# Stage steps ahead of conversions, root-mean-square by token, one output conversion a slot, and attention one slot sooner, in a four-layer kernel on one core

## The reference

```
layer 0 (AB):  y = rms_norm(x) @ w_in; split into a gated linear attention (GLA, 4 heads, dk 128, dv 256)
               and a forgetting attention (8 heads of 128)
    o = gla_chunked(q, k, v, log_a)
    o = o * rsqrt(mean(o*o over dv) + 1e-6) * head_g        # per token and head
    o_gla = o * silu(gate)
    x = x + concat(o_gla, o_fox) @ w_out
layer 1 (C):   u, gate = rms_norm(x) @ w_in; z = gelu(s5_ssm(u)); z *= sigmoid(z @ glu_w + b)
               x = x + (z * silu(gate)) @ w_out
layers 2, 3:   proj = rms_norm(x) @ w_in (6160 columns), split into
    ssd branch (16 heads of 64, chunks of 128), rmsnorm over 1024, weight ssd_norm_w
    conformer:  u = a*sigmoid(g); 31-tap causal conv; silu(layernorm(u over 512)) * silu(z)
    attention:  4 heads, difference of two softmaxes, o = rmsnorm(o over 128, subln) * (1 - lambda_init) * silu(z)
    x = x + concat(y_ssd, y_cfm, y_att) @ w_out
```

## Time and profile before

| | us |
|---|---|
| median of 3 runs | 3405.67 |
| the profiled execution | 3409.92 |
| its span | 3408.1 |
| PE busy (matmul) | 3331.7 (98%) |
| DVE busy | 2139.3 (63%) |
| ACT busy | 1245.7 (37%) |
| DMA share of 16 engines, hardware queue | 50.4% |

### The profile page before, as it was taken

How to read it: one execution, slowest core, us unless ns; L and a number is a source line. 1 busy time by engine, 2 the same in 40 slices (tenths; PEclk the granted TensorE clock), 3 DMA queues, 4 the chain that set the end, 5 groups by cost and what they waited for, 6 DMA issues and landing times.

```text
span 3408.1 us, 43449 instructions
## 1 busy us (share of the span) xinstructions
PE 3331.7 (98%) x16066; PEld 2685.1 (79%) x16066; DVE 2139.3 (63%) x3149; ACT 1245.7 (37%) x1933; POOL 121.6 (4%) x84
## 2 busy tenths in 40 slices
PE   8999999999999999899999999998999999999899
PEld 7887887878888888788888887786778888777677
DVE  5665667686765655434273776666756477666774
ACT  4333324454342233323142226324434223532542
POOL 3000000000020000000020000000002000000000
PEclk9999999999999999999999999998999999999999
DMA  5433345576766666555453444444447354444445
GB/s 173 131 116 121 119 133 184 190 252 233 250 245 199 191 196 194 188 173 206 146 185 119 150 138 155 140 158 148 148 152 250 107 176 143 134 145 155 151 155 207
DMA packets 293233, 575.66 MB, mean 169 GB/s; under 512 B 63392, under 2 KB 107168, under 8 KB 293024
## 3 DMA queue, kind: packets, MB, share of 16 engines
q1 hardware_dynamic: 293024, 572.90, 50.4%
HBM read 440.66 MB, written 132.12 MB: 168 GB/s over the span
## 4 chain that ended last, share of the span: by engine, by line
PE 86%; DVE 7%; ACT 2%; DVEq 2%; DMA 2%; issue 1%; SPq 0%; ACTq 0%
PE bank L557 64%; PE bank L556 12%; DMA convert_in<-mix 1%; DVE weights_low L472 1%; PE bank L1990 1%; PE bank L1572 1%; PE bank L1098 1%; ACT weights_high L403 1%; PE bank L736 1%; DVEq L2592 1%; PE bank L1391 1%; PE bank L1595 1%; PE bank L2296 1%; PE bank L1428 1%; DVE act_low L543 0%
## 5 line engine op out<-in xcount | busy, mean ns | idle before, releaser
L557 PE MATMUL bank<-act_high,weights_high 128*128 128x512 f32 x3584 | 1432.4, 400 | 25.1 <-DVE act_low L540 11.1
L557 PE MATMUL bank<-act_low,weights_high 128*128 128x512 f32 x3584 | 1405.4, 392 | 0.0
L472 DVE TENSOR_TENSOR weights_low<-weights_raw,weights_high 128x1024 fp32r<-128x1024 f32 x528 | 655.9, 1243 | 807.0 <-ACT weights_high L403 796.9
L403 ACT ACTIVATE weights_high<-weights_raw 128x1024 fp32r<-128x1024 f32 x528 | 558.4, 1058 | 1468.5 <-PE bank L557 1220.4
L557 PE MATMUL bank<-act_high,weights_low 128*128 128x512 f32 x3584 | 963.1, 389 | 0.0
L557 PEld LDWEIGHTS bank<-act_high,weights_high 128*128 128x128 f32 x3584 | 678.7, 189 | 184.1 <-issue 24.1
L557 PEld LDWEIGHTS bank<-act_low,weights_high 128*128 128x128 f32 x3584 | 678.9, 189 | 138.4 <-issue 2.9
L557 PEld LDWEIGHTS bank<-act_high,weights_low 128*128 128x128 f32 x3584 | 672.7, 188 | 140.1
L556 PE MATMUL bank<-weights_high,act_high 128*128 128x512 f32 x640 | 253.9, 397 | 3.9 <-DVE stream_out L501 3.1
L556 PE MATMUL bank<-weights_high,act_low 128*128 128x512 f32 x640 | 249.3, 390 | 0.0
L2088 DVE SCALAR_TENSOR_TENSOR residual_in<-residual_in,arena 128x512 f32<-128x512 f32 x240 | 182.1, 759 | 20.2 <-issue 1.5
(11 more groups left out here) (325 smaller groups left out, 2644.4 us busy)
## 6 DMA issues: line engine op xcount, KB each, us to landing
weights_raw<-in_w_all SPq DMA_DIRECT2D x528, 512.0 KB, 3.4
convert_in<-mix SPq DMA_DIRECT2D x80, 256.0 KB, 4.0
fm_b<-stream_out SPq DMA_DIRECT2D x72, 256.0 KB, 3.0
mix<-arena SPq DMA_DIRECT2D x64, 256.0 KB, 3.3
x_part<-stream_out SPq DMA_DIRECT2D x48, 256.0 KB, 4.1
residual_in<-x_part SPq DMA_DIRECT2D x48, 256.0 KB, 5.6
x<-stream_out SPq DMA_DIRECT2D x48, 256.0 KB, 5.4
convert_in<-x SPq DMA_DIRECT2D x48, 256.0 KB, 4.0
```

The costliest lines, as they stand in the source:

```text
L403: e.activation(WH[:, t % 3, :], RAW[:, t % 3, :], ACT.Copy).then_inc(wh_ready, 1)
L472: e.tensor_tensor(WL[:, t % 3, :], RAW[:, t % 3, :], WH[:, t % 3, :].bitcast(F32), ALU.subtract).then_inc(wl_ready, 1)
L557: return e.matmul(bank[s][:, :], a[:, s * P:(s + 1) * P], h, start=start, stop=stop)
```

## The change

- ACT runs `take(t)` before the conversions of the slot, and in slots after a gated pass it converts the weights t+2 first and applies silu or sigmoid after (`late`).
- DVE runs `take(t)` before the conversions in the slots outside `STAGE_FIRST` (in those the stages were first already). The scaling by the ssd norm leaves `convert_dve` and is done one slot before its conversion, ahead of `take` (`scale_dve`); SP loads those blocks two slots ahead.
- The three norms work by token on 4 values a partition, like `stat_*`: one-column sums, root and reciprocal of 128x4, a broadcast copy (`spread`), a product with the identity (`cast`). The multiplications are put in another order.
- `ATT_START` becomes 88 + 6h, `att_pre` moves from slot 84 to 83, and with `ATT_START` the conversions of k = 12 to 15 and the slots in `feeds_pe`.
- The conversions k = 0 to 11 of phases 6 and 8 lie one a slot, in slots 89 to 100.
- PE's first GLA level waits for the last head's `mix1` instead of `mean`; the first logits of a layer wait for the conformer's `t3` instead of `var`.

The diff shows the norms once: the sums and the cast in `gla_pe` (in `cfm_norm_pe` and `att_pe` alike, with one set of columns for each of the conformer's 4 tiles), the rest in `att_dve` (`gla_dve` alike; `cfm_norm_dve` adds up its 4 sets with a tensor_reduce first). Its last part is ACT's order; DVE's changes in the same way, with `scale_dve` ahead of `take`.

```diff
-ATT_START = [89 + 6 * h for h in range(4)]
+ATT_START = [88 + 6 * h for h in range(4)]
...
-            put(B[l] + (90 + k // 2 if k < 8 else 96 + (k - 8) // 2), 6 + 2 * l, k)
+            put(B[l] + 89 + k, 6 + 2 * l, k)
...
+        def scale_dve(e, n):
+            _, ph, k = CONVS[n]
+            x = CV[:, n % 4, :]
+            e.wait_ge(cv_in[n % 4], 16 * (n // 4 + 1))
+            e.scalar_tensor_tensor(x, x, SSDW[(ph - 6) // 2][:, k:k + 1], RS, ALU.mult, ALU.mult).then_inc(conv_h, 1)
...
-            for a in range(2):
-                e.wait_ge(*a_.at(f"square{a}", t))
-                mm = e.matmul(mid[0][:, :], ONES[:, :], gl_sq[:, a, :], start=a == 0, stop=a == 1)
+            e.wait_ge(*a_.at("square1", t))
+            for b in range(TB):
+                for a in range(2):
+                    mm = e.matmul(mid[0][:, b:b + 1], gl_sq[:, a, b * P:(b + 1) * P], ONES[:, 0:1], start=a == 0, stop=a == 1)
             mm.then_inc(*p.mark("sum"))
             yield
             yield
+            e.wait_ge(*d.at("spread", t))
+            for b in range(TB):
+                mm = e.matmul(mid[0][:, b * P:(b + 1) * P], gl_m[:, b * P:(b + 1) * P], IDENT[:, :], start=True, stop=True)
+            mm.then_inc(*p.mark("cast"))
...
-            e.tensor_scalar(at_m, mid[1][:, :], 1.0 / P, EPS, m, add).then_inc(*d.mark("mean"))
+            e.tensor_scalar(at_st, mid[1][:, 0:TB], 1.0 / P, EPS, m, add).then_inc(*d.mark("mean"))
             e.wait_ge(*a_.at("rootv", t))
-            e.reciprocal(at_m, at_m)
-            yield
-            e.drain()
-            e.scalar_tensor_tensor(at_sq, mid[0][:, :], at_sub[:, 0:1], at_m, m, m)
-            e.drain()
+            e.reciprocal(at_st, at_st)
+            e.drain()
+            e.tensor_copy(at_m.rearrange("p (b n) -> p b n", b=TB),
+                          at_st.rearrange("p (b o) -> p b o", o=1).broadcast_to([P, TB, P])).then_inc(*d.mark("spread"))
+            yield
+            e.wait_ge(*p.at("cast", t))
             e.wait_ge(at_zin, 16 * (l * 4 + h + 1))
-            e.scalar_tensor_tensor(at_sq, at_sq, at_li[:, 1:2], at_z, m, m).then_inc(*d.mark("mix"))
+            e.scalar_tensor_tensor(at_sq, mid[1][:, :], at_li[:, 1:2], at_z, m, m)
+            e.drain()
+            e.scalar_tensor_tensor(at_sq, mid[0][:, :], at_sub[:, 0:1], at_sq, m, m).then_inc(*d.mark("mix"))
...
-                if t - 1 in ENDS:
+                late = t - 1 in ENDS and PASSES[ENDS[t - 1]].gate
+                if t - 1 in ENDS and not late:
                     evac_act(e, ENDS[t - 1])
                 if t + AHEAD < NU:
                     weights_act(e, t + AHEAD)
+                if late:
+                    evac_act(e, ENDS[t - 1])
+                take(t)
                 for n in BY_SLOT.get(t, ()):
                     convert_act(e, n)
-                take(t)
```

More of the change, by code:

```diff
@@ L1176, in gla_act @@
             e.wait_ge(*d.at("mean", t))
-            e.activation(gl_m, gl_m, ACT.Sqrt).then_inc(*a_.mark("root"))
+            e.activation(gl_st, gl_st, ACT.Sqrt).then_inc(*a_.mark("root"))
             yield
@@ L2034, in build @@
         cf_cd = steps("cf_conv_dve", "pad") , steps("cf_taps_dve", "v")
-        cf_p, cf_a = steps("cf_pe", "mean"), steps("cf_act", "sq0 sq1 sq2 sq3 root u0 u1 u2 u3")
-        cf_d = steps("cf_dve", "c0 c1 c2 c3 var t0 t1 t2 t3 y0 y1 y2 y3")
+        cf_p, cf_a = steps("cf_pe", "mean cast"), steps("cf_act", "sq0 sq1 sq2 sq3 root u0 u1 u2 u3")
+        cf_d = steps("cf_dve", "c0 c1 c2 c3 var spread t0 t1 t2 t3 y0 y1 y2 y3")
         CD = [dram(f"cfm_conv{l}", [4, P, L]) for l in range(2)]
@@ L2121, in cfm_norm_pe @@
                 e.wait_ge(*cf_a.at(f"sq{k}", l))
-                mm = e.matmul(mid[1][:, :], ONES[:, :], cf_sq[:, k % 2, :], start=k == 0, stop=k == 3)
+                for b in range(TB):
+                    mm = e.matmul(mid[1][:, k * TB + b:k * TB + b + 1], cf_sq[:, k % 2, b * P:(b + 1) * P], ONES[:, 0:1],
+                                  start=True, stop=True)
                 mm.then_inc(*cf_pv.mark("sum"))
             yield
+            e.wait_ge(*cf_d.at("spread", l))
+            for b in range(TB):
+                mm = e.matmul(mid[1][:, b * P:(b + 1) * P], cf_m[:, b * P:(b + 1) * P], IDENT[:, :], start=True, stop=True)
+            mm.then_inc(*cf_p.mark("cast"))
             yield
@@ L2179, in build @@
         at_la, at_ld = steps("at_lambda_act", "exp"), steps("at_lambda_dve", "dot tables")
-        at_p = [steps(f"at_pe{n}", "tq tk l30 l31 l20 l21 l1 t3 tb t1 out sum") for n in range(2)]
+        at_p = [steps(f"at_pe{n}", "tq tk l30 l31 l20 l21 l1 t3 tb t1 out sum cast") for n in range(2)]
         at_a = [steps(f"at_act{n}", "square root q k e30 e31 e20 e00 e21 e01 c3 e10 e11 cb c1 squarev rootv") for n in range(2)]
-        at_d = [steps(f"at_dve{n}", "qr ss kr mx30 mx31 mx20 mx00 mx21 mx01 w3 w2 w0 mx10 mx11 w1 mean mix") for n in range(2)]
+        at_d = [steps(f"at_dve{n}", "qr ss kr mx30 mx31 mx20 mx00 mx21 mx01 w3 w2 w0 mx10 mx11 w1 mean spread mix") for n in range(2)]
         A = Arena(MID_ATT, B_END)
@@ L2331, in att_pe @@
             e.wait_ge(*a_.at("squarev", t))
-            e.matmul(mid[1][:, :], ONES[:, :], at_sq, start=True, stop=True).then_inc(*p.mark("sum"))
+            for b in range(TB):
+                mm = e.matmul(mid[1][:, b:b + 1], at_sq[:, b * P:(b + 1) * P], ONES[:, 0:1], start=True, stop=True)
+            mm.then_inc(*p.mark("sum"))
             yield
+            e.wait_ge(*d.at("spread", t))
+            for b in range(TB):
+                mm = e.matmul(mid[1][:, b * P:(b + 1) * P], at_m[:, b * P:(b + 1) * P], IDENT[:, :], start=True, stop=True)
+            mm.then_inc(*p.mark("cast"))
             yield
```

66 lines of the change are left out of this document (39 added, 27 removed).

## The result

The changed kernel takes 3372.45 us (median of 4 runs, 3369.25 to 3375.03), the kernel before 3408.07 beside it (4 runs, 3402.72 to 3411.36): a ratio of 0.9897, 95% interval 0.9878 to 0.9915. Predicted were 3362 us, and 3343 to 3388. The profiled execution took 3375.03 us, 34.9 less than that of before; the sum had said 43.2.

A forecast was written before the change was run, and what follows sets the result against it. PE, busy 3331.7 of 3408.1 us, was taken as the bound. Gains of 25 + 10.1 + 10.6 + 3.0 + 4.4 less 9.9 made 43.2 us, from 3409.9 to 3366.7, less 4.2 for the median: 3362 us, range 3343 to 3388.

The forecast's parts named there:

- the likeliest case: The forecast of 3362 us with its own spread of 3352 to 3374, given a chance of 0.55.
- First attention heads: Layers 2 and 3: starting a slot sooner with one conversion a slot gains 14 and 11, together 25 us.
- The walk: Layer 2's first head, step by step: PE waits 1.8 us for `spread`, 2.9 for block 3's weights, 2.0 for `w1`.
- what stands behind DVE's new wait for the bank: Attention: the next head's q rotation ends some 3 us after the unit; PE's transpose comes 7.8 us after it.
- Rival 4: Eight early evacuations park DVE at the bank, next head's rotation comes too late for PE: 3419 us, chance 0.06.
- Evacuations: Layer 2's attention: four passes evacuated while their last unit runs, gaining idle 6.9 and clock 3.2, 10.1 us.
- Layer 1: End of its state-space stages: stage copy no longer behind a conversion waiting for DMA, gain 10.6 us (6 to 11.6).
- Output of layer 0: DVE's weights t+2 come before two conversions, so evacuation is less late: 3.0 us gained of 2.0 + 1.6.
- GLA borders: Between GLA heads: idle time behind DVE's reciprocal counted as gone, 4.4 us gained.
- PE's work: Norm sums: 192 one-column passes and 14 casts replace 24 wide sums, adding 9.9 us (5 to 14).
- Rival 3: One-column passes cost only the issue floor, PE's work falls by some 4 us: 3348 us, chance 0.03.
- `late` and the conversions k = 10 and 11: ACT's silus after weights: zero, -3 to +3 us; tight second-head conversions: 0 to 2 us per layer, counted 0.

The follow-up runs named there:

- steps_then_evac: Changed kernel, but in slot 95 of layers 2 and 3 DVE runs the stage steps ahead of the early evacuation: 3360.92 us, ratio 0.9862.
- old_norms: Changed kernel with the norms as before (512-column sums, reciprocals of 128x512), new order and sooner start kept: 3372.81 us, ratio 0.9886.
- order_only: Kernel before with the new order and conversion placement alone, norms and ATT_START as before: 3373.74 us, ratio 0.9889.
- order_norms: Changed kernel without the sooner start (ATT_START 89, att_pre at 84): 3378.12 us, ratio 0.991.
- sooner_only: Kernel before with the sooner start alone (ATT_START 88, att_pre at 83): 3419.02 us, ratio 1.002.
- norms_only: Kernel before with the three norms by token alone, order, conversions and ATT_START as they were: 3410.82 us, ratio 0.9999.
- wide_between: Changed kernel with one unused 128x496 product added between the second and third group of the conformer's one-column sums: 3374.97 us, ratio 0.9901.

## Why the prediction was right, and where it was not

The direction and the range held, and the time lies at the upper edge of the likeliest case (3352 to 3374); the point was 10 us too low. Some of that closeness is luck: layer 1 gave 3.6 us more than its term, which covers part of what the first heads (5.5) and the start of layer 3 (4.7) took. Term by term, in the order of its sum, against the table (gains positive):

- **First attention heads, 25.** By place 15.2. With the work of the conformer's norm (1.3: passes and cast against the old sums) and one head's (0.83) in each layer the gross is 19.5. The walk itself was too dark: no wait for `spread`, 1.0 for block 3's weights instead of 2.9, 1.3 for `w1` instead of 2.0. What it missed is the wait one step further, 3.37 us for the head's square, with the sums and 8 matmuls at 1.2 GHz behind it: 5.9 us in each layer by these rows; steps_then_evac gave back 5.8 and 4.7 there. The step of the prediction that failed is its sentence on what stands behind DVE's new wait for the bank. It followed the next head's rotation to PE's transpose, found time to spare, and stopped. The same rotation feeds a reduction for which ACT waits in order, and ACT's queue holds what PE wants. Rival 4 had the mechanism right, in 2 places of 8 and by another route, and these 10.5 us are its share. Without that wait the gross would have been 30 and not 25, since the walk was too dark elsewhere.
- **The start of layer 3, no term.** 4.7 us. The prediction read the new order only for conversions that run behind attention's stages; that small weights, too, are a stage step that can wait for a DMA (6.26 us on ACT) or for ACT (4.67 on DVE) with conversions behind it was not looked at. The diff shows it: `take` moved ahead of conversions in every slot.
- **Evacuations, 10.1** in layer 2. The rest of layer 2's attention gained 8.6 with the norms' work inside, and 10.6 in old_norms without it. The sooner start is shown to be the cause by the pairs that differ in it alone: 11.4 with the old norms (order_only), 13.8 with the new ones (order_norms). By itself, in sooner_only, it gave 3.3, so the term holds only together with the new order.
- **Layer 1, 10.6.** 14.2, the same in every kernel with the new order and absent without it. The steps are right, the clock was undersized: 8.7 of it is idle time, as the term has it, which leaves 5.5 for the clock where 2.7 were counted. The stretch's mean is 1.00 where it was 0.88.
- **Output of layer 0, 3.0.** 2.8 by place, and that the two are so near is luck. Read finer in the same traces, units 104 to 114, where this evacuation lies, gained 4.1 us in every kernel with the new order; 1.5 of it was lost behind the wait at unit 80, where the clock fell in this execution and not in that of before. norms_only gained 2.4 in 104 to 114 with the old order, so the order is not the only way there.
- **GLA borders, 4.4.** By place 1.2, and 1.3 in old_norms, whose norms are the old ones. So GLA's norms by token free about as much idle time as their four casts cost (4 x 0.83), some 3.3 of the 4.4. The 1.3 are the new order's, which the prediction did not count here: in units 40 to 80 the order alone gained 1.8 us, the norms alone 0.7, both together 1.2.
- **PE's work, 9.9.** 11.7 (3334.6 against 3322.9 in old_norms, some of it the clock behind the conformer's passes). One pass is 0.114 us in the run of 32 (2292.90 - 2289.26 = 3.64), where the conformer's four old sums took 3.22 and not the 3.44 that the prediction counted; a head's norm takes 0.83 more. Rival 3 is out: by it norms_only would have come to 3395, and it stands at 3410.8. The 25 ns of the Trainium skill ("TensorE: Matmul & The Clock Gate", section "Back-to-back issue gap") are given there for matmuls by themselves, and the section says of them that they under-count where each matmul loads weights. So the prediction's words that the skill says otherwise are too strong; these passes load weights each, and take 0.10 to 0.114 us.
- **`late` and the conversions k = 10 and 11, 0.** No wait for the low part L546 is on the list of after; in order_only it is there with 1.3 us in 2 waits. `late` was not run by itself and stays open.

Of the sentences on what would show it: idle time fell to 38 and not 30, the busy time grew by 2.9, the rotation of k has no wait, and L1625 has none. The wait for the weights of block 3 is 1.0 us and not 2 to 4. The adds keep 1.2 us, 0.6 of it behind layer 2's attention, where it was before. One sign of being wrong came up by its letter: `act_low` is on top of the list of waits. It is the 11.1 us ahead of the first unit, which stood second in the list of before, behind the 16.1 for the rotation of k, and which the prediction had set aside; the sign should have left them out.

What the sum hid is the share of each part. It gave the new order, the norms and the sooner start one common term of 25 us. The runs part them: the order alone is worth 0.9889, the whole change 0.9897. The norms are worth nothing, because what they free on DVE, PE pays (16.3 us less idle, 16.4 more busy in norms_only). The sooner start gains 11.4 to 13.8 us in the rest of layer 2's attention and loses most of it at the two first heads; with the evacuation of slot 95 behind the steps, the first heads stand within 1.2 us of those without the sooner start (-15.4 and -10.3 against -16.6 and -10.7 in order_norms).

## What to carry to other kernels

Where one engine is at 98% and the others wait for it in fixed order, the order of the others' queues is a good first thing to change: here the order alone gave what the whole change gave. When an instruction is made to wait, follow every consumer of what is queued behind it, through the other engines' in-order queues, until the bound engine is reached. One that stops at the first consumer with time to spare finds the change free. When steps are moved ahead of others in every slot, list the slots where the moved step itself waits for a DMA.

Cheaper work on an idle engine at the price of work on the bound one pays only by the waits that go with it. Try it place by place: here one of three norms paid.

## What the runs showed of the hardware

- A run of one-column matmul passes was followed by the lower granted clock without any idle time of PE. 32 of them in 3.64 us, with PE never idle ahead, were followed by 8 matmuls at 1.2 GHz, and so it was, with 7 to 14, in 20 places of 20; the same sums over 512 columns in 3.2 us were not, in 8 places of 8.
- One such pass took 0.10 to 0.114 us: 8 of them 0.81 us (L2356), 32 of them 3.64 (L2135), against 3.22 for the conformer's four sums over 512 columns in the kernel before.
- Whether a short idle time costs clock is not fixed. At unit 80 PE waits 1.9 us for L485: in the changed kernel 8 matmuls at 1.2 GHz followed, in steps_then_evac and wide_between none, and the stretch 80 to 204 is 1.8 us shorter there. This alone moves a run by 0.05%.
